# Three inverse square roots of 128x4 in the second block's mixer: a power on GpSimd in place of ScalarE's root and VectorE's reciprocal

## The reference

```
def gmlp_group(u, v, norm_w, ws, bs):
    u = jax.nn.gelu(u).reshape(B, nc, CHUNK, H_A, HEAD_DIM)
    v = rmsnorm_2(jax.nn.gelu(v), norm_w).reshape(B, nc, CHUNK, H_A, HEAD_DIM)
    w = jnp.where(causal[None], ws, 0)
    sv = jnp.einsum('hts,bcshd->bcthd', w, v) + bs.T[None, None, :, :, None]
    return (u * sv).reshape(B, S, D_A)
```

## Time and profile before

| | us |
|---|---|
| median of three runs | 2551.03 |
| profiled execution | 2550.66 |
| its span | 2548.6 |
| PE busy | 2520.1 (99%) |
| POOL busy | 1519.3 (60%) |
| DVE busy | 1326.6 (52%) |
| ACT busy | 567.2 (22%) |

### The profile page before, as it was taken

How to read it: one execution, slowest core, us unless ns; L and a number is a source line. 1 busy time by engine, 2 the same in 40 slices (tenths; PEclk the granted TensorE clock), 3 DMA queues, 4 the chain that set the end, 5 groups by cost and what they waited for, 6 DMA issues and landing times.

```text
span 2548.6 us, 33133 instructions
## 1 busy us (share of the span) xinstructions
PE 2520.1 (99%) x11989; PEld 2065.1 (81%) x11989; DVE 1326.6 (52%) x1566; ACT 567.2 (22%) x1033; POOL 1519.3 (60%) x858
## 2 busy tenths in 40 slices
PE   9999999999999999999999999999999988999998
PEld 7888888778888888888887778888887776888887
DVE  5555427657555315555137666555236656655512
ACT  2110014552111001110015552110013564111000
POOL 6666666436666666666675536666664322666664
PEclk9999999999999999999999999999999989999999
DMA  5332322112322232232232113233223111332232
GB/s 174 99 97 93 99 93 79 53 48 93 99 99 93 97 99 94 96 99 96 95 98 67 59 50 98 92 122 98 94 97 132 59 34 34 99 99 93 97 99 75
DMA packets 66149, 228.75 MB, mean 90 GB/s; under 512 B 8720, under 2 KB 11408, under 8 KB 65680
## 3 DMA queue, kind: packets, MB, share of 16 engines
q1 hardware_dynamic: 64496, 225.67, 27.1%
q10 hardware_dynamic: 1568, 1.88, 0.2%
HBM read 225.43 MB, written 2.10 MB: 89 GB/s over the span
## 4 chain that ended last, share of the span: by engine, by line
PE 97%; DVE 2%; ACT 1%; issue 0%; DVEq 0%; ACTq 0%
PE bank L620 28%; PE bank L622 28%; PE bank L621 28%; PE bank L648 2%; PE bank L807 2%; PE bank L792 2%; PE bank L654 1%; PE bank L776 1%; PE bank L777 1%; PE bank L1038 1%; PE bank L1053 1%; PE bank L1030 0%; PE bank L1029 0%; PE bank L946 0%; PE bank L639 0%
## 5 line engine op out<-in xcount | busy, mean ns | idle before, releaser
L584 POOL TENSOR_TENSOR wl<-raw,wh 128x1024 fp32r<-128x1024 f32 x412 | 1036.8, 2516 | 36.3 <-DVE xl L1660 2.0
L579 POOL TENSOR_SCALAR wh<-raw 128x1024 fp32r<-128x1024 f32 x412 | 444.7, 1079 | 974.3 <-PE bank L622 934.4
L620 PE MATMUL bank<-xh,wh 128*128 128x512 f32 x2088 | 815.2, 390 | 0.0
L621 PE MATMUL bank<-xl,wh 128*128 128x512 f32 x2088 | 813.3, 390 | 0.0
L622 PE MATMUL bank<-xh,wl 128*128 128x512 f32 x2088 | 813.1, 389 | 0.0
L622 PEld LDWEIGHTS bank<-xh,wl 128*128 128x128 f32 x2088 | 391.9, 188 | 82.7
L620 PEld LDWEIGHTS bank<-xh,wh 128*128 128x128 f32 x2088 | 392.0, 188 | 80.8
L621 PEld LDWEIGHTS bank<-xl,wh 128*128 128x128 f32 x2088 | 392.0, 188 | 80.6
L620 PE MATMUL bank<-acth,wh 128*128 128x512 f32 (+1 forms) x902 | 346.4, 384 | 0.0
L621 PE MATMUL bank<-actl,wh 128*128 128x512 f32 (+1 forms) x902 | 346.2, 384 | 0.0
L622 PE MATMUL bank<-acth,wl 128*128 128x512 f32 (+1 forms) x902 | 346.2, 384 | 0.0
(11 more groups left out here) (293 smaller groups left out, 2379.6 us busy)
## 6 DMA issues: line engine op xcount, KB each, us to landing
raw<-in_stream SPq DMA_DIRECT2D x412, 512.0 KB, 3.6
w1k<-in_w1k SPq DMA_DIRECT2D x1, 2048.0 KB, 9.0
x<-in_x SPq DMA_DIRECT2D x3, 512.0 KB, 6.5
w1v_low<-in_w1v SPq DMA_DIRECT2D x1, 1024.0 KB, 7.0
w1v_high<-in_w1v SPq DMA_DIRECT2D x1, 1024.0 KB, 9.0
out_dram<-x SPq DMA_DIRECT2D x4, 256.0 KB, 2.6
out_dram<-x SPq DMA_DIRECT2D x1, 768.0 KB, 3.7
x<-in_x SPq DMA_DIRECT2D x2, 256.0 KB, 5.3
```

Source lines behind the costliest of these rows:

```text
L579: nc.gpsimd.tensor_scalar(wh[:, h, :, :], src, 1.0, 1.0, ALU.mult, ALU.mult)\
L584: nc.gpsimd.tensor_tensor(wl[:, h, :, :], src, wh[:, h, :, :].bitcast(F32), ALU.subtract).then_inc(split_done, 1)
L620: mm = nc.tensor.matmul(bank, wh[:, slot, k, :], rh, start=start, stop=False)
L621: mm = nc.tensor.matmul(bank, wh[:, slot, k, :], rl, start=False, stop=False)
```

## The change

The lists of step numbers are moved into named tables (`AT_PE`, `AT_ACT`, `AT_DVE`, `AT_POOL`), with the same numbers as before, and the order of `shared` is built from them. ACT's two kinds of root go, among them the root of a constant behind step 63, and DVE's two reciprocals of `gss` and `rs4`. POOL raises the means to the power -0.5 in place, against a tile of 128x4 that holds -0.5. The powers stand in POOL's program behind the split of unit 16 (gate), of unit 18 (first output norm) and of unit 20 (second), and each waits for its means. For that the first six turns of POOL's loop over the second model (24 units) are written out. The consumers wait for the powers' semaphores: ACT's scaling of the gate for `gv_rstd`, DVE's spread for `rs_part`. `square_b` and `add_blocks` state their waits in a general form. A new tile `halves` of 16 bytes a partition stands ahead of `room`, so that the tiles declared behind it lie further on.

```
+AT_POOL = dict(gv=16,
+               a=18,
+               b=20)
...
+        halves = sb("halves", [P, NQ])
         room = sb("room", [P, 8])
...
-            with pool.Fori(U_BLOCK2 // 4, U_ALL // 4) as i:
+
+            def powers(n, u):
+                for name, at, ready, done in (("gv", gss[:, :], gv_mean, gv_rstd), ("a", rs4[:, 0, :], mean2, rs_part),
+                                              ("b", rs4[:, 1, :], mean2, rs_part)):
+                    if u == U_BLOCK2 + AT_POOL[name]:
+                        pool.wait_ge(ready, 2 if name == "b" else 1)
+                        pool.wait_ge(halves_set, 1)
+                        nc.gpsimd.tensor_tensor(at, at, halves[:, :], ALU.pow).then_inc(done, 1)
+
+            nc.gpsimd.memset(halves[:, :], -0.5).then_inc(halves_set, 1)
+            for i in range(U_BLOCK2 // 4, U_BLOCK2 // 4 + 6):
+                split_units(i, powers)
+            with pool.Fori(U_BLOCK2 // 4 + 6, U_ALL // 4) as i:
                 split_units(i)
...
-            def root_of(n):
-                act.wait_ge(mean2, n + 1)
-                nc.scalar.activation(rs4[:, n, :], rs4[:, n, :], ACT.Sqrt).then_inc(root2, 1)
...
-                if G == 38:
-                    act.wait_ge(gv_mean, 1)
-                    nc.scalar.activation(gss[:, :], gss[:, :], ACT.Sqrt).then_inc(gv_root, 1)
+                if G == AT_ACT["gv_root"]:
                     for c in range(NQ):
                         scale_gated(c)
...
-                if G == 50:
-                    root_of(0)
...
-            nc.scalar.activation(first_root[:, :], ones[:, 0:1].bitcast(F32), ACT.Sqrt)
             copy_turn2(STEPS2 - 3)
             copy_turn2(STEPS2 - 2)
             spread2(7)
             copy_turn2(STEPS2 - 1)
             numerators2(7)
             square_b(3)
-            root_of(1)
...
             def token_inverse(n):
-                dve.wait_ge(root2, n + 1)
-                V.reciprocal(rs4[:, n, :], rs4[:, n, :]).then_inc(rs_part, 1)
                 dve.wait_ge(rs_part, n + 1)
...
-                if G == 38:
+                if G == AT_DVE["gv_mean"]:
                     dve.wait_ge(gsq_done, NQ)
                     V.tensor_scalar(gss[:, :], gss[:, :], 1.0 / 512, EPS, ALU.mult, ALU.add).then_inc(gv_mean, 1)
-                    dve.wait_ge(gv_root, 1)
-                    V.reciprocal(gss[:, :], gss[:, :]).then_inc(gv_rstd, 1)
```

More of the change, by code:

```diff
@@ L95 @@
 STEPS2 = 64
-FILL2 = tuple(2 + (G in (9, 12, 15, 18, 21, 24, 27, 29, 31, 33, 35, 37, 39, 40)) if G < 41 else (1, 1, 3, 3)[G - 41]
-              if G < 45 else 0 for G in range(STEPS2))
+FILL2 = (2, 2, 2, 2, 2, 2, 2, 2, 2, 3, 2, 2, 3, 2, 2, 3, 2, 2, 3, 2, 2, 3, 2, 2, 3, 2, 2, 3, 2, 3, 2, 3, 2,
+         3, 2, 3, 2, 3, 2, 3, 3, 1, 1, 3, 3, 0, 0, 0, 0, 0, 0, 0, 0, 0, 0, 0, 0, 0, 0, 0, 0, 0, 0, 0)
+AT_PE = dict(values1=10,
+               gate_turn=3,
+               hidden=7,
+               hidden_turn=12,
+               keys=14,
+               block_values=16,
+               scores=(22, 24, 38, 48),
+               weights=(30, 54),
+               blocks=(32, 39, 56, 62),
+               gated=(33, 34, 35, 36),
+               spatial=(40, 41, 42, 43),
+               a_sums=49,
+               a_rows=52,
+               out=(56, 57, 58, 59, 60, 61, 62, 63))
+AT_ACT = dict(queries=(13, 26, 46),
+               exp=(26, 50),
+               copy=(31, 55),
+               gelu_v=30,
+               squares=(34, 35, 36, 37),
+               square_b=(38, 41, 58),
+               gv_root=38,
+               gelu_u=42,
+               square_a=(46, 46, 47, 47),
+               a_root=50,
+               high=(54, 54, 55, 55))
+AT_DVE = dict(inverse=(9, 10, 11, 13),
+               residual=(17, 18, 20, 21, 24, 26, 30, 31),
+               queries=(12, 25, 45),
+               low_q=(14, 27, 47),
+               keys=15,
+               gv=(16, 19, 22, 29),
+               values=17,
+               mask=20,
+               bias=(23, 25, 39, 49),
+               minimum=(25, 49),
+               normalise=(28, 51),
+               blocks=(33, 40, 57, 63),
+               gu=(32, 35, 38, 41),
+               copy=(34, 35, 36, 37),
+               gv_mean=38,
+               spatial=(40, 41, 42, 43),
+               add_b=(43, 59),
+               gated=(45, 45, 46, 46),
+               add_a=(47, 48, 48),
+               a_mean=50,
+               a_inverse=51,
+               normed=(53, 53, 54, 54),
+               low=(55, 55, 56, 56))
+AT_POOL = dict(gv=16,
+               a=18,
+               b=20)
 OUT_BANK = (0, 1, 2, 5, 3, 4, 7, 6)
@@ L104, with shared_order @@
 EVACUATED = {2: 1, 3: 2, 0: 3, 1: 4, 4: 5, **{n: n + 1 for n in range(5, U_PROJ2)}}
[L107 to L110, removed]
+def shared_order():
+    order = ["gate_sums"]
+    for G in range(STEPS2):
+        v, s = divmod(G, 8)
+        order += ["values0"] * (G == 1) + ["gate_turn"] * (G == AT_PE["gate_turn"]) + ["hidden"] * (G == AT_PE["hidden"])
+        order += ["values1"] * (G == AT_PE["values1"]) + ["hidden_turn"] * (G == AT_PE["hidden_turn"])
+        order += [f"rows{v - 1}"] * (s == 5 and v > 0)
+        order += ["keys"] * (G == AT_PE["keys"]) + ["block_values"] * (G == AT_PE["block_values"])
+        for name in ("scores", "weights", "blocks", "gated", "spatial"):
+            order += [f"{name}{n}" for n, at in enumerate(AT_PE[name]) if at == G]
+    return order + ["rows7", "sums", "norm_rows"]
+SHARED = shared_order()
 def written(name):
@@ L326, in build @@
         fin_set = sem("fin_set")
[L327 removed]
+        x_in = {m: sem(f"x_in{m}") for m in (0, 1, 3, 5, 7)}
         gains_in = sem("gains_in")
@@ L1516, in _ @@
                     numerators2(v - 1)
[L1517 to L1525, removed]
+                for n, at in enumerate(AT_ACT["exp"]):
+                    if at == G:
+                        compressed_exp(n)
+                for n, at in enumerate(AT_ACT["queries"]):
+                    if at == G:
+                        high_q2(n + 1)
```

179 lines of the change are left out of this document (87 added, 92 removed).

## The result

The changed kernel took 2570.86 us (median, 2569.7 to 2571.65) against 2551.09 us (2548.9 to 2551.74) for the kernel before: 1.0080 times as long, with a 95% interval of 1.0067 to 1.0092. The forecast was 2548.8 us and its range ended at 2552.5. The change costs some 20 us where it was expected to give 2 or cost nothing.

The account below looks back on a forecast made before the run. TensorE, busy 99% of the span, was taken as the bound. Terms -0.9 and -1.5, of which 1.9 is left at the first norm, then +0.5, -0.4, -0.1 gave -1.9 from 2550.66: 2548.8 us, range 2545.0 to 2552.5.

Parts of the forecast that it names:

- so only four things change: Second block's mixer: three roots and reciprocals become powers, three splits slip, three VectorE waits and one early table load go.
- Power: Each 128x4 power on GpSimd: taken as 0.7 us, with 0.1 below and 2.4 above.
- Gate norm, -0.9: Step 38: VectorE's addition and means come sooner, the root wait goes, and TensorE's 0.9 us bias wait goes whole.
- Gating, -1.5: Steps 45 to 48: first gating pair falls from 2.81 to 1.28 us, halving TensorE's 3.1 us stall.
- First output norm, -1.9 left: Steps 48 to 52: means come 2.4 + 1.0 us earlier, 1.3 us is paid back, 1.9 us of gain is left.
- The collision: First output norm: unit 19's split falls into VectorE's softmax products and spread, paying back 1.3 us; TensorE stalls up to 4.
- The clock, +0.5: Steps 52 to 63: clock falls at the new 4 us stall, so the slow stretch moves; 0.5 us charged.
- Second norm and the load, -0.1 and -0.4: Second output norm: the power gains 0.1 us; the table load at 2130.32 goes, gaining 0.4 us.
- A: Rival, first output norm and steps 48 to 57: clock holds and splits miss VectorE; 2545.0 us, chance 0.17.
- B: Rival, second output norm first: the power is slow; at 8 us the kernel takes 2560.4 us; chance 0.07.
- C: Rival: stalls only change names, clock stays low until step 60, moved split takes the rest; 2550.3 us, chance 0.28.
- the forecast as worked out: Whole kernel: the summed terms' own case, 2547.2 to 2550 us, chance 0.48.

Follow-up runs that it names:

- e1: Changed kernel without the spare tile `room`, so `halves` takes its place and all tiles behind lie at the old addresses; 2549.65 us against 2550.32, ratio 0.9996.
- e2: Kernel before with `room` 32 bytes a partition larger, every tile behind it 32 bytes further on, no powers; 2568.89 us, ratio 1.0075.
- e9: Kernel before with 32 more spare bytes ahead of everything, so all tiles, weights and streamed alike, begin 32 bytes later; 2550.02 us, ratio 1.0000.
- e5: Changed kernel without `room`, GpSimd's splits of units 19 and 21 held until VectorE has spread the factors; 2547.61 us against 2550.44, ratio 0.9987.
- e6: Kernel before with its spare 32 bytes set ahead of `wh`: weights and small tiles behind them move, streamed tiles stay; 2611.25 us, ratio 1.0236.
- e11: Kernel before with `acth` and `actl` moved alike by 256, 512, 1024, 160 and 128 bytes in the five feed-forwards; 2557.23 us, ratio 1.0029.
- e3: Kernel before with `room` 64 bytes a partition larger, so every tile behind it begins 64 bytes later; 2557.67 us, ratio 1.0030.
- e4: Kernel before with 32 bytes ahead of `acth` and 32 more behind it, so `acth` stands 32 and `actl` 64 bytes off; 2567.12 us, ratio 1.0066.
- e8: Kernel before with separate places for `acth` and `actl` in each of five feed-forwards, the two moved by different distances in some; 2564.31 us, ratio 1.0052.

## Why the prediction was wrong, point by point

e1 has the addresses that the prediction was worked out for, so its trace is read against the terms.

**The step that failed** is the list on which the sum rests: "so only four things change". A fifth did: the tile `halves` moves what stands behind it, 32 bytes off the weights, and some 3,150 matmuls of 512 columns over those tiles (858 x 3 over `acth` and `actl`, 192 x 3 over `mh` and `ml`) pay some 6 to 7 ns each, 6.67 in the down stages. The diff showed the tile, yet the prediction gave the move no term, no bound and no rival, so no part of its range could hold it. e1 and e2 show the cause from both sides: the change without the move costs nothing that the runs can tell, the move without the change costs as much as the changed kernel lost. The trace of before had no row with its price; a bound would have had to come from the number of matmuls that stream moved tiles.

**Power.** 1.02 to 1.04 us each; taken at 0.7, bounds 0.1 and 2.4. The first was no dearer than the others, and its consumer on ScalarE started at 2058.30, 0.06 us behind its end in e1. In the profile a power is the same operation, TENSOR_TENSOR, as the split's subtraction ahead of it.

**Gate norm, -0.9.** Right. In e1 the addition takes 0.69 us, the means come at 2056.96 (2056.9 was said), the scalings start at 2058.30 (2058.36), and the spatial product at 2066.01 in place of 2066.86.

**Gating, -1.5.** Right, the pair by 1.5 and the rows behind it: TensorE in e1, against 2088.89 with 3.14 us (2089.20 in e9) and 2086.5 with 1.6 us forecast (the rows under the first are for what follows):

```profile
2086.51 0.47 PE L1102 MATMUL bank<-kh,qs 128*128 128x512 f32 x1 [1.62 <-issue]
...
2103.74 0.63 PE L1061 MATMUL bank<-ident,scc 128*128 128x128 f32 x4 [2.23 <-DVE on L2042]
...
2140.26 0.66 PE L1154 MATMUL bank<-ident,bsb 128*128 128x128 f32 x4 [0.52 <-DVE bsb L2142]
```

**First output norm, -1.9 left.** Nearly right: the copy ends at 2099.22 where 2098.8 was said. It ended at 2100.77 before and at 2100.35 in e9, which has no power and only lies 32 bytes further on as a whole, so the gain is 1.1 to 1.6 us. The collision is as described; of the 0.42 us by which the copy is late, the size of the power (1.02 for 0.7) makes 0.32. That the split leaves the softmax reduction free, as the -1.9 takes it, no row of the trace before shows. In e1 the reduction at 2095.16 kept its 0.69 us under the split's product, which ran until 2095.69, so leaving it free was the right choice. The two-input product behind it took 1.99 us under the split's subtraction (0.17 in e5, without it). The stall was 1.43 us, not up to 4.

**The clock, +0.5.** These runs cannot price the term. Behind the stall of 1.62 us, where the clock "may hold", it fell: in e1 it is 0.50 from 2088.5 to 2098. The windows of e1 (length, busy us by engine, granted clock, DMA):

```profile
2088.50:2098.00 9.50, 8.94 (x47) 7.19 (x45) 7.63 (x18) 4.72 (x13) 4.28 (x3) 0.50 0.01 2
...
2080.00:2100.00 20.00, 15.26 (x102) 12.52 (x101) 16.95 (x39) 12.36 (x33) 4.41 (x3) 0.74 0.03 10
2100.00:2120.00 20.00, 16.45 (x114) 13.14 (x113) 12.29 (x32) 12.92 (x36) 0.00 (x0) 0.91 0.05 18
2120.00:2140.00 20.00, 17.66 (x119) 13.62 (x117) 7.01 (x12) 5.88 (x17) 5.50 (x4) 1.00 0.09 27
2140.00:2160.00 20.00, 17.46 (x70) 13.70 (x71) 14.50 (x16) 5.81 (x10) 10.05 (x6) 0.91 0.18 58
```

and of e9, which has no power, with three rows of its timelines that are wanted here and below:

```profile
2080.00:2100.00 20.00, 15.22 (x100) 12.84 (x99) 16.01 (x38) 14.04 (x36) 3.41 (x2) 0.77 0.08 28
2100.00:2120.00 20.00, 16.07 (x119) 12.88 (x119) 13.21 (x35) 14.99 (x39) 0.00 (x0) 0.98 0.00 1
...
2140.00:2160.00 20.00, 17.54 (x72) 13.69 (x71) 14.73 (x16) 5.87 (x10) 7.76 (x6) 0.91 0.19 59
...
2099.92 0.43 DVE L2089 COPY bsb<-rs 128x512 f32<-128x512 f32 x1
...
2105.08 0.63 PE L989 MATMUL bank<-ident,scc 128*128 128x128 f32 x4 [2.23 <-DVE on L1986]
...
2138.77 1.58 DVE L2089 COPY bsb<-rs 128x512 f32<-128x512 f32 x1
```

With a clock of 0.5 in the slow part and 1.0 elsewhere, the half-clock time between 2080 and 2120 is (0.26 + 0.09) x 20 / 0.5 = 14.0 us in e1 against (0.27 + 0.15) x 20 / 0.5 = 16.8 before, but only (0.23 + 0.02) x 20 / 0.5 = 10.0 us in e9. The rows at 2103.74 are 2.4 us ahead of 2106.14, but 1.3 us ahead of e9's. And from 2140 to 2160, where the execution before stood at full clock, e1 and e9 alike have 0.09 x 20 / 0.5 = 3.6 us at half clock. In e1 a stall of 1.8 us for `ml` (L2152) at 2148.94 stands ahead of it, but the kernel before has that stall too, and the clock held:

```profile
PE bank L620 <- DVE ml L2098: 2.3, 2, 1.8
...
2140.00:2160.00 20.00, 17.52 (x78) 13.64 (x79) 15.25 (x16) 5.23 (x9) 9.90 (x5) 1.00 0.16 53
```

So the time at half clock differs by 6.8 us between two executions without a power. What part of the clock's course is owed to the change stays open.

**Second norm and the load, -0.1 and -0.4.** The 0.58 us wait is gone. The split caught the copy: means to the copy's end take 2.63 us against 2.28, +0.35 in place of -0.1.

```profile
2137.57 0.16 DVE L2138 TENSOR_SCALAR rs<-bank 128x4 f32<-128x4 f32 x1 [2.95 <-PE bank L1232]
...
2138.87 1.05 POOL L640 TENSOR_SCALAR wh<-raw 128x1024 fp32r<-128x1024 f32 x1
...
2138.92 1.28 DVE L2142 COPY bsb<-rs 128x512 f32<-128x512 f32 x1 [1.19 <-POOL rs L670]
```

The copy ends at 2140.20, 2.5 us earlier than before, but in e9 it ends at 2140.35: at this point the gain cannot be told from the clock's course. The span of e1 is 1.0 us shorter than before, where -1.9 was said, and its times (0.9996, interval through 1) cannot tell either from nothing. Of the rivals, A and B did not occur: the clock fell, and the powers took 1.0 us. C (2550.3) and the forecast as worked out (2547.2 to 2550) stand too near each other for e1's 2549.65 to decide between them.

**Open.** How the price follows from the distances (3.52, 1.19, 3.51 and 4.01 us a down stage at 32, 64, 128 and 160 bytes, 3.10 in the shorter last one at 96), and what makes it, is not settled. That the distance to the weights alone is enough, e6's gate stages show (+7.01 us); whether two streamed tiles that stand apart cost more by that, no run separates.

## What to carry to other kernels

A new tile is an edit to every tile that is allocated behind it: read the diff's declarations as you read its instructions, and put a small new tile behind the large ones, or pad it (a move by 256 bytes cost nothing in e11, one by 32 or 128 some 3.5 us a down stage). In this kernel, keep the tiles that matmuls stream and the tiles of their weights at the same place within 256 bytes. When a local change moves the whole kernel's time, compare the mean of the largest groups first, before the place of the edit; 6 ns on thousands of matmuls is easy to overlook in a mean of 390. Before a row of one execution is put down to a change, look for the same row in a run without it, as e9 served here. And a split that GpSimd may run at leisure can be held until the short VectorE work on the path is over, which made the row product of e5 start 1.5 us sooner.

## What the runs showed of the hardware

- A 512-column matmul of this kernel starts 227 ns behind the one before where the streamed tiles and the weights stand alike within 256 bytes, and on average over the three products of a down stage 229 to 234 ns behind it at the distances run where they don't, at the same granted clock of 1.0 (e2 to e11).
- All of them moved by 32 bytes together cost nothing (e9: 389 ns, as before). Where a tile's neighbour in the sequence stands counts too: a matmul over `actl` 64 bytes on takes 388 ns with `acth` 64 bytes on (e3) and 394 with `acth` 32 on (e4), and the next matmul starts on average 232 ns behind one over an unmoved `acth` when `actl` stands 32 bytes on (e8), against 227 before.
- A power of 128x4 on GpSimd takes 1.02 to 1.04 us (the changed kernel).
- GpSimd's one-input split product holds VectorE's copy as well: 1.28 us in place of 0.43 (e1 against e5), and its two-input subtraction held a product of 128x16, 1.99 us in place of 0.17. A reduction beside the one-input product kept its 0.69 us (e1).
- The time at half clock in the second model's mixer varies without any change: 16.8 us between 2080 and 2120 in the kernel before, 10.0 in e9.
